# Key norms and bonus sums of a recurrent scan, moved from each head into the gates' stage

## What is computed

```python
kk = _heads(k * k_k)
kk = kk * lax.rsqrt(jnp.sum(kk * kk, axis=-1, keepdims=True) + 1e-12)    # key norms, per token and head
k_mod = k[None] * (1 + (a - 1) * k_a)                                    # per direction z
...
S = S * w_t + sa * b_t + v_t * k_t                                       # the scan, step by step
...
bonus = einsum('bthk,zbthk->bth', _heads(r) * r_k, _heads(k_mod))        # per token and head, both directions
y = layernorm(y, ln_g, ln_b) + bonus[..., None] * _heads(v)
gate = sigmoid(xg @ g1) @ g2
out = (y * gate) @ wo
```

## Time and profile before

| | |
|---|---|
| median of 3 runs | 4155.14 us (4152.47 to 4157.6) |
| the profiled execution | 4159.04 us, its span 4157.2 us |
| PE, DVE, ACT, POOL busy | 3742.9, 2460.3, 1220.1, 1327.0 us of the span |

### The profile page before, as it was taken

One profiled execution on the slowest core, in us unless ns is written; L12 is line 12 of the kernel. 1 busy time (PEld: TensorE's weight loads), 2 busy tenths in 40 slices (PEclk: granted clock), 3 DMA queues, 4 the chain that ended last, 5 costly groups with the idle time before them and its releaser, 6 DMA issues. The chain is left out here.

```text
span 4157.2 us, 81021 instructions
## 1 busy us (share of the span) xinstructions
PE 3742.9 (90%) x32324; PEld 2658.9 (64%) x32324; DVE 2460.3 (59%) x3950; ACT 1220.1 (29%) x2692; POOL 1327.0 (32%) x1020
## 2 busy tenths in 40 slices
PE   8889999898999999886999997996999999689887
PEld 7667778656887888773444446754888887533332
DVE  4559973546984455564444447735988886633333
ACT  3352223343222322330111113223554544111111
POOL 4544443433445264660000001412554543000000
PEclk9999999999999999997999998997999999799999
DMA  4115542303453222427999991545232323299997
GB/s 127 52 53 194 177 148 71 96 13 137 173 194 112 84 64 71 131 90 298 420 420 420 420 420 65 191 150 150 63 81 56 80 73 143 105 393 421 421 421 321
DMA packets 228732, 781.49 MB, mean 188 GB/s; under 512 B 55464, under 2 KB 63480, under 8 KB 168672
## 3 DMA queue, kind: packets, MB, share of 16 engines
q1 hardware_dynamic: 222544, 757.93, 49.2%
q0 software_dynamic: 5328, 19.40, 1.2%
q10 hardware_dynamic: 576, 0.09, 0.0%
HBM read 730.06 MB, written 47.28 MB: 187 GB/s over the span
## 5 line engine op out<-in xcount | busy, mean ns | idle before, releaser
L2965 ACT ACT_TABLE_LOAD x32 | 41.1, 1283 | 540.4 <-PE moe0e_p_u L2918 272.2
L2863 POOL DMA_INDIRECT moe0e_xg<-moe_h,moe_first_rows x20 | 19.3, 966 | 560.6 <-DVE moe_first_rows L2998 552.8
L3860 PE MATMUL scan_bank<-scan_T,scan_off 64*64 64x64 f32 x3840 | 164.5, 224 | 37.3 <-issue 21.9
L1227 DVE SCALAR_TENSOR_TENSOR f0u_ada<-hT,condition,f0u_ada 128x512 f32<-128x512 f32 x168 | 196.9, 1242 | 0.4 <-DVE f0u_ada L1227 0.4
L1227 DVE SCALAR_TENSOR_TENSOR f1u_ada<-hT,condition,f1u_ada 128x512 f32<-128x512 f32 x168 | 173.2, 1100 | 6.3 <-DMA hT<-in_ada_w_dram 5.8
L373 POOL TENSOR_TENSOR gmi_w_lo<-gmi_rows_w,gmi_w_hi 128x512 fp32r<-128x512 f32 x64 | 120.3, 1880 | 161.8 <-ACT gmi_w_hi L415 161.8
L3860 PEld LDWEIGHTS scan_bank<-scan_T,scan_off 64*64 64x64 f32 x3840 | 141.3, 139 | 46.0 <-issue 27.1
L2918 PE MATMUL moe0e_p_g<-moe_ring,moe0e_xT 128*64 128x512 f32 x608 | 163.7, 614 | 1.0 <-issue 1.0
L373 POOL TENSOR_TENSOR p_w_lo<-p_rows_w,p_w_hi 128x512 fp32r<-128x512 f32 (+3 forms) x88 | 113.6, 1293 | 158.8 <-ACT p_w_hi L415 158.8
L2863 POOL DMA_INDIRECT moe1e_xg<-moe_h,moe_first_rows x17 | 16.3, 960 | 459.7 <-DVE moe_first_rows L2998 452.8
L2918 PE MATMUL moe1e_p_g<-moe_ring,moe1e_xT 128*64 128x512 f32 x512 | 135.7, 608 | 28.7 <-DMA moe_ring<-in_moe_w_gu_dram 27.7
(11 more groups left out here) (880 smaller groups left out, 11467.9 us busy)
## 6 DMA issues: line engine op xcount, KB each, us to landing
moe_ring<-in_moe_w_gu_dram SPq DMA_DIRECT2D x280, 1024.0 KB, 16.3
moe_ring<-in_moe_w_down_dram SPq DMA_DIRECT2D x140, 1024.0 KB, 15.9
hT<-in_ada_w_dram SPq DMA_DIRECT2D x48, 1024.0 KB, 6.3
f0u_w<-in_ffn_w_gate_up_dram SPq DMA_DIRECT2D x22, 1024.0 KB, 4.8
f1u_w<-in_ffn_w_gate_up_dram SPq DMA_DIRECT2D x22, 1024.0 KB, 4.9
gmi_rows_w<-in_ga_w_in_dram SPq DMA_DIRECT2D x64, 256.0 KB, 2.8
gmo_w<-in_ga_w_out_dram SPq DMA_DIRECT2D x64, 256.0 KB, 2.9
p_rows_w<-in_ab_w_in_dram SPq DMA_DIRECT2D x48, 256.0 KB, 2.7
```

Source lines behind the costliest of these rows:

```text
L1227: ins = V.scalar_tensor_tensor(out=acc[:, z, :], in0=src, scalar=cond[:, n * HALF + k, z:z + 1], in1=acc[:, z, :], op0=ALU.mult, op1=ALU.add)
L2863: pool.indirect_dma_start(xg[:], None, H.h, bass.IndirectOffsetOnAxis(rows[:, 0:1], 0)).then_inc(gathered, 16)
L2965: nc.scalar.activation(sg[:], p_g[:], ACT.Silu).then_inc(silu_ready, 1)
L3860: mm = nc.tensor.matmul(out[r], lhsT[r], rhs[r], start=start, stop=stop, skip_group_check=True)
```

## The change

The norms and the bonus sums no longer belong to a head of the scan. The gates' stage reads k and r back from DRAM (into `xx` and `hT`, after the last mix), makes squares and products of whole blocks of 128 channels, that is of two heads, and sums them on TensorE with two columns, one for each half (`norm_of`, `plain_of`, `rate_of`). Its slots run decay, rate, gate. Norm sums stand behind each rate pair, bonus sums behind each two gate slots. The ring has 3 places instead of 4, the gate is stored in 4 pieces. The results are kept in SBUF (`rw_inverse`, `rw_token_bonus`). In the scan the square, norm, `rk` and bonus instructions go; the bonus rows are loaded as v and GpSimd multiplies and shifts them by token tile, one instruction a head in heads 2 to 9. SP issues `sides` and `sg` first and the tables of the heads after the loads of head 0.

```diff
 def rwkv_gates(...)
-    MIX, RING = 4, 4
+    MIX, RING = 4, 3
         slots = [("w", d, z) for d in range(KD) for z in range(2)]
+        slots += [("a", d, z) for d in range(KD) for z in range(2)]
         slots += [("g", j, q) for j in range(NT) for q in range(2)]
-        slots += [("a", d, z) for d in range(KD) for z in range(2)]
 # SP
+                sp.wait_ge(mixed, len(LOW) * KD)
+                for q in range(2):
+                    sp.dma_start(keys[:, 4 * q:4 * q + 4, :], kF[0]...).then_inc(k_loaded[q], 16)
+                for q in range(2):
+                    sp.dma_start(products[:, 4 * q:4 * q + 4, :], rF[0]...).then_inc(r_loaded[q], 16)
 # VectorE, for each block d
+                V.tensor_tensor(squares[d % 2][:], keys[:, d, :], keys[:, d, :], ALU.mult)
+                V.tensor_tensor(products[:, d, :], products[:, d, :], keys[:, d, CTX:], ALU.mult)
+                    V.tensor_tensor(chunked(both[d % 2]), chunked(f[0]...), backward(f[1]...), ALU.add)
+                    V.tensor_tensor(shares[:, d, :], both[d % 2], products[:, d, :], ALU.mult)
 # TensorE
+                def norms(d):
+                    for n in range(STEPS):
+                        for half, step in ((lo, n), (hi, mirrored(n))):
+                            mm = nc.tensor.matmul(ss_psum[half, 2 * d:2 * d + 2, step], squares[d % 2][:, n * CH:(n + 1) * CH], norm_of[:, d, :], ...)
+                def bonus(d):
+                    for t in range(NT):
+                        nc.tensor.matmul(o, products[:, d, rows], plain_of[:, d, :], start=True, stop=False, ...)
+                        mm = nc.tensor.matmul(o, shares[:, d, rows], rate_of[:, d, :], start=False, stop=True, ...)
+                        if kind == "a":
+                            norms(d)
+                    if kind == "g" and z == 1:
+                        for n in (2 * d, 2 * d + 1):
+                            bonus(n)
 def rwkv_scan(...)
 # SP
-                for dst, src in ((masks, ...), (join, ...), (eye, ...), (keep, ...), (sides, ...), (cols_all, ...)):
+                sp.dma_start(sides[:], a["rw_sides"]).then_inc(s["const_loaded"], 16)
                 load_sg(0)
+                for dst, src in ((keep, ...), (cols_all, ...)):
                 load(0)
+                load_tables()
                 load_v(0)
                 load_v(1)
                 load_raw(0)
+                load_bonus()
 # GpSimd, behind the factors of the head ahead
+                    if 2 <= h < 2 + 2 * NT:
+                        bonus_part(h - 2)
 # ScalarE
-                        A(sq[:], k2[:], ACT.Square, scale=cols(h, 0)).then_inc(s["sq_ready"], 1)
 # VectorE
-                        c.step(V.tensor_scalar(ss[:], ss_bank, 1e-12, None, ALU.add))
-                        c.mark(V.reciprocal(w[h % 3][:], ss[:]))
-                        c.mark(V.scalar_tensor_tensor(out=rk[:, i], ...))
-                    V.tensor_copy(bon[:], bon_psum).then_inc(s["bon_read"], 1)
-                    add_bonus()
                     split_block()
-                    add_shift()
 # TensorE
-                            mm = mmul(ss_bank[:, j:j + 1], sq[:, j * CH:j * CH + CH], S.ones[:, 0:1])
                     turn(1)
-                    bonus(0)
                     part(walk_solve, 2)
-                    bonus(1)
                     part(walk_share, 2)
```

More of the change, by code:

```diff
@@ L4025, in body @@
                         walk_part(2 * n + 1)
-                        if ahead is not None:
-                            factor_part(ahead, n)
-                for slot in range(SLOTS):
-                    factor_part(0, slot)
                 heads(body)
-FACTOR_STEPS = 12
+FACTOR_STEPS = 8
 def rwkv_tables():
@@ new lines, in copy_gate @@
+                def copy_gate(j):
+                    for q in range(2):
+                        s = 4 * KD + 2 * j + q
+                        dve.wait_ge(summed, s + 1)
+                        V.tensor_copy(gt[:, j, q * BANK:(q + 1) * BANK], ring[s % RING][:, 0:BANK]).then_inc(copied, 1)
+                for d in range(KD):
+                    if d + 2 < KD:
+                        square(d + 2)
+                    share(d)
+                dve.wait_ge(norm_summed, KD)
+                V.tensor_scalar(ss[:], ss_psum, 1e-12, None, ALU.add).then_inc(norm_step, 1)
@@ L4608, in _ @@
+                dve.wait_ge(norm_step, 1)
+                V.reciprocal(S.rw_inverse[:], ss[:]).then_inc(norm_step, 1)
+                for j in range(NT):
+                    copy_gate(j)
+                dve.wait_ge(bonus_summed, KD)
+                V.tensor_copy(S.rw_bonus[:], bonus_psum)
             @block.scalar
```

206 lines of the change are left out of this document (124 added, 82 removed).

## The result

The changed kernel takes 4172.59 us (median of 5, 4168.06 to 4175.16) against 4152.77 us before (5 runs, 4149.56 to 4157.6): ratio 1.0044, 95% interval 1.003 to 1.0059, slower by 0.44%. The profiled execution took 4175.16 us, its span 4173.3, 16.1 us more than the span before.

| | before | after | difference | predicted |
|---|---|---|---|---|
| start of the program to the first decay pair | 2779.2 | 2773.5 | -5.7 | 0 |
| gates' stage, to the scan's first DMA issue | 59.8 | 102.9 | +43.1 | +26.5 |
| scan, to the first mask of head 0 | 24.1 | 22.0 | -2.1 | -5.5 with head 0 |
| head 0 | 39.8 | 37.3 | -2.5 | |
| heads 1 to 14 | 558.8 | 541.6 | -17.2 | -8.5 |

A forecast was written before the change was run, and what follows sets the result against it. No engine bounds a whole scan head (TensorE and VectorE alternate); TensorE decides the gates' stage. Gates' stage +26.5 us and scan -14 us give +12.5 on 4155.1, about 4168 us, range 4149 to 4182.

The forecast's parts named there:

- Decay slots, ring of 3: Gates' stage: with three ring places a pair waits for ScalarE, 2.5 us against 1.74, bounds 1.74 and 2.6.
- rival 4: Gates' stage: the smaller ring costs nothing, decay slots keep 1.74 us, 6 us less, 4162; chance 0.05.
- Price of a norm record: Gates' stage, rate slots: 0.055 us for each of 48 records a pair, 2.64 us; rate slots 33 us.
- rival 1: Gates' stage: column halves load weights in parallel, 0.0275 us a norm record, 10.6 us less, 4157; chance 0.20.
- Gate slots and bonus sums: Gates' stage, TensorE: eight gate slots 16.9 us plus 128 bonus records 13.9 us, 30.8 us in all.
- Rival 3: Heads and decay slots: half clock more often, head gain of 10 gone and 3 us more, 4181; chance 0.13.
- Start of the scan and head 0: Earlier `sg` and `lw` loads and less VectorE work in the first head: -5.5 us, bounds -3 and -8.
- ss and reciprocal: Scan heads, VectorE: without them `at_rt` starts ahead of `kh`; 1.0 us in 10 heads, -10 us.
- Bonus work in the heads: Scan heads: removing TensorE's bonus matmuls and VectorE's bonus work gains 0; an earlier 0.1 to 0.2 us taken as 0.
- Bonus rows on GpSimd: Heads 2 to 9: eight added instructions of 2.4 us each, costing +1.5 us, bounds 0 and 6.
- Rival 2: Scan: heads bound by TensorE throughout, 14 heads give 32 us instead of 10, 4146; chance 0.13.

The follow-up runs named there:

- run 7: Changed kernel with bonus sums made with 128x64 weights in alternating partition halves, 256 records instead of 128: gates' stage 89.6 us, one execution 4154.68 us.
- run 5: Changed kernel with the 384 norm records of the gates' stage left out: stage 96.3 us, one execution 4160.45 us.
- run 1: Kernel before with VectorE's ss and reciprocal left out of the scan: 39.06 us a head against 39.91, one execution 4145.40 us.
- run 2: Kernel before with all bonus work left out of the scan, norms kept: 39.33 us a head against 39.91, one execution 4165.94 us.
- run 3: Kernel before with only TensorE's 32 bonus records a head left out: 39.74 us a head against 39.91, one execution 4175.58 us.
- run 4: Kernel before with TensorE's 48 norm records a head left out of the scan: 39.89 us a head, one execution 4147.15 us.
- run 8: Changed kernel with norms behind decay pairs, bonus records in 128x64 halves behind rate pairs, gate slots last: median 4147.3 us, ratio 0.9992 to the kernel before.

## Why the prediction came out right, and which steps did not

The median lies 4.6 us above the forecast of 4168, on the side that was forecast, but that it lies so near is luck. The forecast was 12.5 us above the kernel before, and the medians differ by 19.8. By stage, 26.8 us too little in the gate slots stand against 9.1 us too much for the norm records, some 8 us too little gain in the scan, and 5.7 us ahead of the first decay pair that are not the change. The direction hangs on the same miss: by these rows the gates' stage would take 43.1 - 26.8 = 16.3 us more at full clock, an estimate, and the scan gains 21.8. The forecast had the right stage growing, but the half clock that made the kernel slower was not in its sum.

- *Decay slots, ring of 3.* 2.5 us a pair taken, 2.6 the bound; measured 2.61. Right; rival 4 is out.
- *Price of a norm record.* 0.055 taken, 0.0275 in rival 1; measured 1.49 / 48 = 0.031. The step that failed is the reading of the 16 records with 128x64 weights, that they speak against parallel halves. They alternate between the halves of the output, as the norm records do (L744 writes `ps_o[half(u), ...]` for u = 0, 1), and they show the halves side by side. What follows them in the kernel before are full records with the same 128 moving columns:

```profile
198.29 0.66 PE L785 MATMUL em_ps_g<-identity,em_e_l 128*128 128x128 f32 x4
198.78 0.38 PE L732 MATMUL em_ps_t<-identity,em_probs 128*128 128x128 f32 x2
```

  Four full ones take 198.78 - 198.29 = 0.49 us, 0.12 each, and the 16 halves 198.29 - 197.26 = 1.03 us, 0.064 each. In the single records of that trace the halves start two at a time, 0.005 us apart, with 0.109 us from pair to pair, the same as from one full record to the next. So 0.055 was half the price of 128 moving columns, and not the price of 64 columns of weights. The norm records have two moving columns; there the pairs follow at 0.06 us. The rate phase is 23.9 us, not 33: 9.1 us less. The page "TensorEngine Tiling (Array Packing)" of the Trainium skill (Key Properties) says that different tiles can load weights and multiply in parallel; this trace and run 7 agree. The page "TensorE: Matmul & The Clock Gate" of the Trainium skill (Part 3, The mechanism) lets a weight load overlap with running matmuls only where the row group differs; here both tiles use all rows, and 0.031 us a record does not agree with it.
- *Gate slots and bonus sums.* 16.9 + 13.9 = 30.8 us at full clock; measured 57.6. The records cost what they were taken for as long as the clock was up (in run 5, 2815.00 - 2814.54 = 0.46 us for four, 0.115 each). The step that failed is that all of this was summed at full clock, without a reason given. Rival 3 had half clock in the heads and in the decay slots, for 13 us in all; it came in the gate slots, for 26.8 us. By this sum the stage would be 76 us without it and the whole 4146 us, an estimate, 0.17% below the kernel before, which is no difference that can be told.
- *Start of the scan and head 0.* -5.5 forecast, -4.6 measured.
- *ss and reciprocal.* -10 forecast from 10 heads; -11.9 in run 1. Right, and its mechanism too (2.10 to 0.58 us), with a remainder that was not foreseen: the second product takes 0.6 us longer.
- *Bonus work in the heads.* 0 forecast; -8.1 in run 2. TensorE's part is 0 (run 3), the norm records 0 (run 4); VectorE's is 0.58 us a head. The prediction saw 0.1 to 0.2 us of the earlier start, measured 0.28, and dropped it. It did not see that the scan of decays gets shorter: GpSimd makes its row of joins (ten in 8.68 us before, in 8.11 after) beside it, and a VectorE instruction with two inputs in SBUF stretches there, as `at_rt` does beside `kh`. That this is the reason for 0.96 and 0.67 us is argued, not shown; no run moved the joins alone.
- *Bonus rows on GpSimd.* 1.90 and 2.36 us each against 2.4 (the estimate by columns); +1.5 forecast. In run 8 the eight heads with one of them are 38.4 us in the mean, as are the six others: 0.
- *Rival 2* (heads bound by TensorE, 39.9 - 2.3 = 37.6 us) did not come: 38.1 in the shortest head. But the scan's gain of 21.8 us, against the 14 that were forecast, lies on its side.

## What to carry over

Ask of a sum not only how many records but at which clock they run: here the same gate slots and bonus records cost about double, in the tail of a stage, where nothing hides it. Give matmuls with few output columns 64-column weights and let them alternate between the halves of the partitions; the same sums took half the time in run 7. A small instruction is worth its place and not its length: 0.39 us ahead of a neighbour engine's long one gave 0.85 us a head, while 48 records in a hole gave nothing.
